# Output norms with the channel weight applied at tile read-out and two paired steps, and one scan term moved ahead, in a two-block fp32 kernel

## What is computed

```python
def rms_norm(x, g):
    xf = x.astype(jnp.float32)
    y = xf * lax.rsqrt(jnp.mean(xf * xf, axis=-1, keepdims=True) + RMS_EPS)
    return (y * g.astype(jnp.float32)).astype(x.dtype)

        mix = hybrid_mixer(rms_norm(h, g_pre_mix[layer]), ...)
        h = h + rms_norm(mix, g_post_mix[layer])
        ffn = conv_gated_mlp(rms_norm(h, g_pre_ffn[layer]), ...)
        h = h + rms_norm(ffn, g_post_ffn[layer])
```

```python
    y = y_diag + y_off + d_skip[:, :, None] * x_c
    return y.reshape(b, L, G * E * P)
```

## Time and profile before

| | |
|---|---|
| median of three executions | 834.76 us (834.15 to 835.37) |
| the profiled execution | 834.96 us, of which span of the profile 833.1 us |
| PE busy | 821.7 us (99%), 6800 matmuls |
| DVE busy | 619.2 us (74%), 1029 instructions |
| ACT busy | 504.1 us (61%), 875 instructions |
| POOL busy | 128.8 us (15%) |
| granted PE clock | 9 (tenths) or more in every one of 40 slices |

### The profile page before, as it was taken

How to read it: one execution, slowest core, us unless ns; L and a number is a source line. 1 busy time by engine, 2 the same in 40 slices (tenths; PEclk the granted TensorE clock), 3 DMA queues, 4 the chain that set the end, 5 groups by cost and what they waited for, 6 DMA issues and landing times.

```text
span 833.1 us, 16905 instructions
## 1 busy us (share of the span) xinstructions
PE 821.7 (99%) x6800; PEld 796.6 (96%) x6800; DVE 619.2 (74%) x1029; ACT 504.1 (61%) x875; POOL 128.8 (15%) x128
## 2 busy tenths in 40 slices
PE   8999999999999999999999999999999999999997
PEld 8999999999999999999999999999998999889896
DVE  6647998877666689767664478999888696568765
ACT  6446666555444576555554368787968554356655
POOL 1000000000000305443441100043515010000002
PEclk9999999999999999999999999999999999999999
DMA  8754435345565536655666625645545375654321
GB/s 305 268 158 138 157 108 173 127 153 180 190 187 181 178 100 205 200 181 186 191 195 186 189 95 164 197 141 196 172 140 171 111 233 180 192 165 140 128 101 51
DMA packets 39854, 139.82 MB, mean 168 GB/s; under 512 B 4433, under 2 KB 5089, under 8 KB 39649
## 3 DMA queue, kind: packets, MB, share of 16 engines
q1 hardware_dynamic: 38160, 135.91, 51.0%
q10 hardware_dynamic: 1616, 2.84, 1.0%
HBM read 137.67 MB, written 1.06 MB: 167 GB/s over the span
## 4 chain that ended last, share of the span: by engine, by line
PE 88%; DVE 7%; ACT 2%; POOL 1%; issue 1%; DMA 1%; DVEq 0%; SPq 0%; ACTq 0%; POOLq 0%
PE ps L1858 65%; PE ps L1923 5%; PE ps L1882 4%; PE ps L1861 4%; DVE weights_lo L1117 2%; PE ps L2043 1%; PE ps L2067 1%; PE ps L2328 1%; PE ps L2347 1%; PE ps L2054 1%; PE ps L1885 1%; ACT weights_hi L572 1%; PE ps L1979 1%; PE ps L2336 1%; DMA raw_weights<-weights_in 1%
## 5 line engine op out<-in xcount | busy, mean ns | idle before, releaser
L1117 DVE TENSOR_TENSOR weights_lo<-raw_weights,weights_hi 128x1024 fp32r<-128x1024 f32 x251 | 313.7, 1254 | 84.2 <-ACT weights_hi L572 83.0
L572 ACT ACTIVATE weights_hi<-raw_weights 128x1024 fp32r<-128x1024 f32 x250 | 262.1, 1053 | 142.1 <-issue 65.2
L1858 PE MATMUL ps<-x_hi,weights_hi 128*128 128x256 f32 (+3 forms) x1184 | 340.3, 287 | 0.3 <-DVE arena L1493 0.2
L1858 PE MATMUL ps<-x_lo,weights_hi 128*128 128x256 f32 (+3 forms) x1184 | 333.7, 282 | 0.0
L1858 PE MATMUL ps<-x_hi,weights_lo 128*128 128x256 f32 (+3 forms) x1184 | 333.1, 281 | 0.0
L1858 PEld LDWEIGHTS ps<-x_hi,weights_hi 128*128 128x128 f32 x1184 | 222.8, 188 | 4.5 <-issue 3.1
L1858 PEld LDWEIGHTS ps<-x_lo,weights_hi 128*128 128x128 f32 x1184 | 222.8, 188 | 0.7 <-issue 0.5
L1858 PEld LDWEIGHTS ps<-x_hi,weights_lo 128*128 128x128 f32 x1184 | 223.2, 189 | 0.0
L1858 PE MATMUL ps<-y_lo,weights_hi 128*128 128x256 f32 (+1 forms) x488 | 137.4, 282 | 0.0
L1858 PE MATMUL ps<-y_hi,weights_hi 128*128 128x256 f32 (+1 forms) x488 | 137.3, 281 | 0.0
L1858 PE MATMUL ps<-y_hi,weights_lo 128*128 128x256 f32 (+1 forms) x488 | 137.1, 281 | 0.0
(11 more groups left out here) (285 smaller groups left out, 1195.6 us busy)
## 6 DMA issues: line engine op xcount, KB each, us to landing
raw_weights<-weights_in SPq DMA_DIRECT2D x251, 512.0 KB, 3.7
arena<-decay_rows ACTq DMA_DIRECT2D x8, 256.0 KB, 3.7
masks<-masks_in SPq DMA_DIRECT2D x1, 1202.0 KB, 7.9
raw_weights<-weights_in SPq DMA_DIRECT2D x4, 256.0 KB, 5.4
hidden<-xT_in SPq DMA_DIRECT2D x3, 272.0 KB, 5.8
hidden<-xT_in SPq DMA_DIRECT2D x1, 276.0 KB, 3.1
gate_w<-gate_w_in ACTq DMA_DIRECT2D x1, 256.0 KB, 3.6
out<-arena ACTq DMA_DIRECT2D x1, 256.0 KB, 2.1
```

The lines of the kernel that those rows point to most:

```text
L572: a.sig(A(whi[:, s * CW:(s + 1) * CW], raw[:, (c % RAW) * CW:(c % RAW + 1) * CW], ACT.Copy), "hi_ready")
L1117: d.sig(TT(wlo[:, s * CW:(s + 1) * CW], raw[:, (c % RAW) * CW:(c % RAW + 1) * CW], whi[:, s * CW:(s + 1) * CW].bitcast(F32), ALU.subtract) ...
L1858: ins = mm(bank(BANK_OF[no])[:, 0:b - a], wt, x_[:, kt, a:b], start=s0, stop=s1)
```

## The change

In `out_tiles` the copy out of PSUM becomes a multiplication by the channel weight, and ACT squares the tile in PSUM instead of the copy (the copy now carries the weight, which the mean square must not have). So the bank is free only when ACT has read it, and the table `taken` says `sq_ready` instead of `mout_ready` for tiles 0 to 6. In `post_norm` the product with channel weight and inverse root mean square becomes a product of two tensors. The steps of tiles 3 and 4, and of tiles 5 and 6, are done by one instruction each, on 128 x 2 x 258 (or 256); `normed(1)`, `add(1)` stand directly behind each other, and so do `normed(7)`, `add(7)`. In the scans, `ssd_y(u + 1)` moves ahead of the `ssd_low` steps, of `z_full` and of `z_half`.

```diff
--- before.py
+++ after.py
@@ -401,6 +401,8 @@
                     cnt[name] = 2 * KT
                 cnt[name] = cnt.get(name, 0) + 1
                 taken[FIRST_OUT[s_, i_] + o] = (name, cnt[name])
+                if name == "mout_ready" and i_ < KT - 1:
+                    taken[FIRST_OUT[s_, i_]] = ("sq_ready", (KT if s_ == "wo" else 3 * KT) + i_ + 1)
 
 
         FIRST_HALF = [("eb", 0), ("ec", 0), ("ex", 0), ("ex", 1), ("ex", 2), ("ez", 0), ("eg", 0), ("ex", 3), ("ez", 1),
@@ -722,7 +724,7 @@
                         split_hi()
                     if i < KT - 1:
                         act.wait_ge(S("mout_ready"), n0 + i + 1)
-                        a.sig(A(sq[:, i, t0:T], mout[:, i, t0:T], ACT.Square), "sq_ready")
+                        a.sig(A(sq[:, i, t0:T], bank(BANK_OF[FIRST_OUT[stage, i]])[:, 0:T - t0], ACT.Square), "sq_ready")
                     if i == KT - 2:
                         split_hi()
                 act.wait_ge(S("out_ready"), FIRST_OUT[stage, KT - 1] + 1)
@@ -1301,7 +1303,7 @@
                     d.sig(TT(ylo[:, MERGED, j, :], mm1[:, j % 2, :], yhi[:, MERGED, j, :].bitcast(F32), ALU.subtract),
                           "merged_split")
 
-            def out_tiles(stage, t0, base):
+            def out_tiles(stage, t0, base, gain):
 
                 for i in range(KT):
                     for _ in chunk_of((stage, i))[:-1]:
@@ -1309,11 +1311,11 @@
                     r = result((stage, i), 0, T - t0)
                     if i == KT - 1:
                         dve.wait_ge(S("sq_ready"), base + KT)
-                    d.sig(V.tensor_copy(mout[:, i, t0:T], r), "mout_ready")
+                    d.sig(TS(mout[:, i, t0:T], r, pcol(gain, i), None, ALU.mult), "mout_ready")
                     if i < KT - 1:
                         split_lo()
 
-            def post_norm(nth, gain_post, gain_pre, base, t0):
+            def post_norm(nth, gain_pre, base, t0):
 
                 dve.wait_ge(S("rms_half"), nth // 2)
                 h = (T - t0) // 2
@@ -1325,36 +1327,44 @@
 
                 first = d.n.get("normed", 0)
 
-                def normed(kt):
-                    m = mout[:, kt, t0:T]
-                    d.sig(STT(out=m, in0=m, scalar=pcol(gain_post, kt), in1=rpost[:, t0:T], op0=ALU.mult, op1=ALU.mult),
-                          "normed")
-
-                def add(kt):
-                    dve.wait_ge(S("normed"), first + kt + 1)
-                    d.sig(TT(H[:, kt, t0:T], H[:, kt, t0:T], mout[:, kt, t0:T], ALU.add), "h_ready")
+                def normed(k0, k1):
+                    m = mout[:, k0:k1, t0:T]
+                    r = rpost[:, t0:T].unsqueeze(1).to_broadcast([P, k1 - k0, T - t0])
+                    d.sig(TT(m, m, r, ALU.mult), "normed", k1 - k0)
+
+                def add(k0, k1):
+                    dve.wait_ge(S("normed"), first + k1)
+                    d.sig(TT(H[:, k0:k1, t0:T], H[:, k0:k1, t0:T], mout[:, k0:k1, t0:T], ALU.add), "h_ready", k1 - k0)
 
                 d.settle()
                 for c, (a0, a1) in enumerate(((t0, t0 + h), (t0 + h, T))):
                     m = mout[:, 0, a0:a1]
                     if c:
                         dve.wait_ge(S("rms_ready"), nth)
-                    ins = STT(out=m, in0=m, scalar=pcol(gain_post, 0), in1=rpost[:, a0:a1], op0=ALU.mult, op1=ALU.mult)
+                    ins = TT(m, m, rpost[:, a0:a1], ALU.mult)
                     d.sig(ins, "normed") if c else d.step(ins)
                     d.settle()
                     d.sig(TT(H[:, 0, a0:a1], H[:, 0, a0:a1], m, ALU.add), "h_ready" if c else "h_half")
-                normed(1)
-                for kt in range(1, KT):
-                    if kt + 1 < KT:
-                        normed(kt + 1)
-                    add(kt)
-                    low(kt - 1)
+                normed(1, 2)
+                add(1, 2)
+                normed(2, 3)
+                low(0)
+                add(2, 3)
+                low(1)
+                for k in (3, 5):
+                    normed(k, k + 2)
+                    low(k - 1)
+                    add(k, k + 2)
+                    low(k)
+                normed(KT - 1, KT)
+                add(KT - 1, KT)
+                low(KT - 2)
                 low(KT - 1)
                 split_lo()
                 square_sum(nth * KT, t0)
 
-            out_tiles("wo", TA, KT)
-            post_norm(2, "g_post_mix", "g_pre_ffn", KT, TA)
+            out_tiles("wo", TA, KT, "g_post_mix")
+            post_norm(2, "g_pre_ffn", KT, TA)
             feed(("fu", 0))
             feed(("fg", 0))
             dve.wait_ge(S("rms_ready"), 3)
@@ -1398,8 +1408,8 @@
                 feed(("fu", i))
             ffn_out(FT - 1)
             feed(("fg", FT - 1))
-            out_tiles("fd", META, 3 * KT)
-            post_norm(4, "g_post_ffn", "even_norm", 2 * KT, META)
+            out_tiles("fd", META, 3 * KT, "g_post_ffn")
+            post_norm(4, "even_norm", 2 * KT, META)
             halves = prm[:, PARAMS["even_conv"]:PARAMS["even_conv"] + 50]
             d.step(TS(halves, halves, 0.5, None, ALU.mult))
             gate_b = prm[:, PARAMS["gate_b"]:PARAMS["gate_b"] + 4]
@@ -1653,6 +1663,7 @@
                     conv_rest(("ex", u + 2), u + 2, xs[:, u + 2, :])
                 z_half(("ez", u + 1), zs[:, 1, :])
                 feed(("ez", u + 1))
+                ssd_y(u + 1)
                 if p == 2:
                     ssd_low(2)
                     ssd_low(3)
@@ -1661,7 +1672,6 @@
                 if p < 3:
                     z_full(("ex", u + 2), xs[:, u + 2, :], name="xsilu")
                 z_half(("eg", u + 1), gs[:, (u + 1) % 4, :])
-                ssd_y(u + 1)
                 gla_scores(p)
                 feed(("eg", u + 1))
                 if p < 3:
```

## The result

The changed kernel takes 837.17 us (median of 7 executions, 836.71 to 838.06); the kernel before, run beside it, 834.75. The ratio is 1.0031, with a 95% interval of 1.0021 to 1.0041: slower by some 2.4 us, where 837.2 was forecast. The profiled execution took 837.53 us, its span is 835.7.

A forecast was written before the change was run, and what follows sets the result against it. PE, busy 99% at full clock, was taken as the bound. Two norms at +1.2 us each and 0 for the scan made +2.4 on 834.76, so 837.2, own range 836.5 to 838.2, 8-in-10 range down to 835.0.

The forecast's parts named there:

- Bound: Whole kernel: PE busy 99% at full clock, so only its idle time, taken away or added, changes the time.
- Copies and squares: 0: Copies out of PSUM and ACT's squares while PE still works: longer copy and later bank release cost 0.
- Tile 0: -0.06: First tile of each norm: a shorter `normed` starts the high part and PE 0.06 us earlier per norm.
- The pair: 0.70: Paired `add` of 516 elements on DVE in the norms: takes 0.70 us, the next starts 0.62 later.
- Two standstills of 0.67: First norm: DVE stands still 0.67 us before `low(3)` and again before `low(5)`, until ACT's high part is done.
- `low(7)` 1.22 later, PE 0.8 late by itself, then waiting for the chunk: +1.2: End of each norm: `low(7)` 1.22 us later, PE 0.8 late, then chunk wait before `fg` 1; +1.2 per norm.
- Scan move: 0: Skip term moved in the scans: `turn_x(6)` waits 0.5 us less, `gla_kv` starts unchanged; 0, bounds -0.5 and +0.1.
- Sum +2.4: Whole kernel: 2 x 1.2 for the norms plus 0 for the scan, +2.4 us, median 837.2.
- faster: Rival, 832.3 us: high parts come in time, PE walks at its own pace, `turn_x` wait gained too; chance 0.10.
- Half of it: Rival, 836.4 us: PE does not wait for the `fg` 1 chunk, or ACT is quicker; +1.6, chance 0.14.
- The skip term pays: Rival in the scan, 836.7 us: `turn_x` starts 0.5 us earlier and `gla_kv` with it; chance 0.09.
- The clock falls: Rival, 840 us or more: PE's four standstills within 10 us drop its clock to half; chance 0.02.

The follow-up runs named there:

- singles in the old order: Changed kernel with one product per tile in the norms, in the norm order of the kernel before, the scan as changed; 833.70 us, ratio 0.9992.
- before with low behind: Kernel before with only the remainders (`low`) of tiles 3 and 5 put directly behind their half steps (`add`); 838.51 us, ratio 1.0047.
- the two kernels of singles: Changed kernel with each pair split into single products, once in the norm order of the kernel before (833.70 us), once in the changed order (836.12 us).
- scan only: Kernel before with only `ssd_y(u + 1)` moved as the change moves it; 834.87 us, ratio 1.0004.
- take first: Changed kernel with unpaired norms in the earlier order, scan's gla scores earlier, and at p = 2 `conv_in`, gate product, states before remainders and chunk; 833.37 us.
- norms only: Changed kernel with the skip term `ssd_y(u + 1)` put back where the kernel before has it; 837.20 us, ratio 1.0031.

## Why the prediction was right

- **Bound.** PE at full clock and 98%, and the time moved by what PE's stretches moved. Right.
- **Copies and squares: 0.** The product out of PSUM takes 0.49 us instead of 0.42, DVE is idle 0.56 behind it instead of 0.63, and singles in the old order lose nothing. Right.
- **Tile 0: -0.06.** -0.05, right.
- **The pair: 0.70.** 0.69, and the next starts 0.61 or 0.62 later. Right.
- **Two standstills of 0.67.** They show as 0.58 in brackets each; from the point where DVE could have gone on (298.99 + 0.61 = 299.60) to 300.25 it is 0.65. Right in place and size, and before with low behind shows the standstill with no pair at all. What the step did not set apart is the order (+2.35 in both norms), the shorter products (-0.9) and a pair's late count (+0.9), which the two kernels of singles showed; in the hand calculation all three were in the times of the high parts.
- **`low(7)` 1.22 later, PE 0.8 late by itself, then waiting for the chunk: +1.2.** PE's stretch grew by 1.22 and 1.23. PE's own last matmul group on the tiles began at 305.54, and `fg` 1 at 306.92, 0.15 after the chunk's end (305.55 + 1.22). At some 1.07 us a tile PE was through with the tiles at 306.61, so about 0.9 of the 1.22 was its own lateness and 0.3 the chunk; in the second norm the wait is listed, 0.2 for L1119. Right.
- **Scan move: 0.** That the wait of `turn_x` moves to `gla_kv` and `gla_kv` gains nothing was right (8.07 us against 8.11). The step failed in its frame: it looked at DVE's order up to `gla_kv` and took an unbroken DVE for an unchanged one. The same instructions in another order met GpSimd otherwise: its products end later, the chunk split behind `gla_scores` takes 2.03 us instead of 1.62, and what stands behind it moves on. Counted from `gla_scores(2)`, DVE's product with the gate starts at 11.80 instead of 11.43, the taking of the keys at 18.87 instead of 18.50, GpSimd's next work at 19.42 instead of 19.06, and PE's second start of `ssd_heads(6)` at 31.53 instead of 31.18. The term is +0.35, outside its bounds of -0.5 and +0.1.
- **Sum +2.4.** By the two stretches it would be +2.7, by the profiled executions 837.53 - 834.96 = +2.6, by the medians +2.4. So the hit within 0.1 us is better than the prediction's own steps: the 0.35 of the scan was missing, and that the medians came out 0.3 below the stretches is luck within the noise.

Rivals: *faster* fell by the point that it named, the hand-over behind a pair's `add`. *Half of it* fell: the chunk was waited for. *The skip term pays* fell with scan only. *The clock falls* did not happen: the page shows 9 in all slices, through PE's new waits.

## What to carry to other kernels

Where two engines hand tiles to and fro, count the instructions that stand between giving a tile away and needing the answer: here 0.59 us had to be covered, the old order had 1.05 us between the end of an `add` (298.27) and its `low` (299.32), and taking such cover away on unchanged instructions cost twice 2 us. A paired instruction saved 0.07 us on its own engine here and delayed the first tile for everyone else by 0.27, so pair what nobody waits for. And a wait of the bound engine is worth its length only if no other chain ends just behind it: before spending an edit on one, look for the next wait in the following 20 us, and for the engine that had no gap up to there.

## What the runs showed of the hardware

- DVE instructions with two inputs in SBUF and GpSimd's products, side by side, look as if they took turns. This is read from their lengths, and spans on GpSimd are rough. DVE's split of a chunk is 1.22 us alone and 1.62, 2.02 or 2.03 beside GpSimd's products; GpSimd's L502 is 0.99 to 1.03 alone and 1.72 to 1.82 behind a split; in take first DVE's `z_full` of 0.42 became 1.22 while GpSimd's product, lengthened by the split of 634.42, ran to 634.78 + 1.72 = 636.50; `z_full` ended 0.28 later. DVE instructions that read one input from PSUM kept their length there: 0.47 for the skip term and 0.73 for the masking in the kernel before, both beside GpSimd's products of 613.21 to 615.53. The Trainium skill ("SBUF — State Buffer", section "SBUF: two separate sides", on the port pair that DVE and GpSimd share) says that a DVE operation with two inputs in SBUF and a GpSimd operation that reads SBUF lock each other out for a whole instruction; these lengths agree.
- The consequence for a prediction: swapping instructions on DVE, none added and no gap made, moved what follows by 0.4 us, since another one met GpSimd.
- DVE is busy 619.7 us after the change and 619.2 before, with eight instructions fewer. The longer split is not the whole reason, since norms only, without it, shows 619.5. The sixteen read-outs of the norms cost 0.06 us more each, 1.0 together, against the shorter products and the pairs; the balance was not followed further, and over all kernels here the total lies between 618.7 and 620.3.
